# Two column sets of the first mixing stage as seven block products, with their sums on the POOL queue and VectorE

## What is computed

```
h = rmsnorm(x, g_mix[l])
p = h @ w_in[l]                                  # 1024 -> 5632 columns
gates = sigmoid(p[..., OFF_G:]).reshape(b, s, 3, 1024)
y_f = fourier_mix(p[..., OFF_F:OFF_B], w_fourier[l])
y_c = short_conv(p[..., OFF_B:OFF_C], p[..., OFF_C:OFF_V], p[..., OFF_V:OFF_P], w_conv[l], w_conv_out[l])
y_p = pool_mix(p[..., OFF_P:OFF_G], w_pool[l], pool_scale[l])     # (...) * scale
x = x + (gates[:, :, 0] * y_f + gates[:, :, 1] * y_c + gates[:, :, 2] * y_p) @ w_o[l]
```

## Time and profile before

| | us |
|---|---|
| median of 3 runs | 2215.95 (2215.57 to 2216.9) |
| the profiled execution, device time | 2217.72 |
| its span, first to last instruction | 2215.9 |
| first mixing stage, layer 0 and layer 1 | 175.3 and 175.0 |

### The profile page before, as it was taken

One profiled execution on the slowest core, in us unless ns is written; L12 is line 12 of the kernel. 1 busy time (PEld: TensorE's weight loads), 2 busy tenths in 40 slices (PEclk: granted clock), 3 DMA queues, 4 the chain that ended last, 5 costly groups with the idle time before them and its releaser, 6 DMA issues.

```text
span 2215.9 us, 28791 instructions
## 1 busy us (share of the span) xinstructions
PE 2208.1 (100%) x11494; PEld 1886.2 (85%) x11494; DVE 1729.2 (78%) x2163; ACT 1321.5 (60%) x1489; POOL 56.0 (3%) x68
## 2 busy tenths in 40 slices
PE   9999999999999999999999999999999999999999
PEld 8888888888888888888888888888888888788887
DVE  7887566888788566788888799768788887976787
ACT  6566445556556544666656676555565667754555
POOL 0000000000000000000000000000000000000000
PEclk9999999999999999999999999999999999999999
DMA  7977555977879556698597753549778785345876
GB/s 274 327 224 259 166 185 186 310 224 234 287 245 273 187 172 208 215 300 236 193 321 239 236 171 118 204 160 325 231 234 277 239 261 195 105 162 195 287 244 185
DMA packets 170950, 503.86 MB, mean 227 GB/s; under 512 B 18720, under 2 KB 23328, under 8 KB 162624
## 3 DMA queue, kind: packets, MB, share of 16 engines
q1 hardware_dynamic: 161456, 434.90, 55.1%
q0 software_dynamic: 9216, 67.11, 15.4%
q10 hardware_dynamic: 144, 0.00, 0.0%
HBM read 500.91 MB, written 1.05 MB: 227 GB/s over the span
## 4 chain that ended last, share of the span: by engine, by line
PE 90%; DVE 4%; DMA 4%; ACT 1%; issue 1%; SPq 0%; ACTq 0%; DVEq 0%
PE psum L756 24%; PE psum L757 12%; PE psum L692 12%; PE psum L694 12%; PE psum L693 12%; PE psum L888 4%; PE psum L892 4%; PE psum L890 4%; DMA raw<-t_gate_up_1a_dram 2%; DVE split_w L1843 2%; PE psum L724 2%; DMA raw<-t_gate_up_2a_dram 1%; PE psum L1115 1%; DVE gate_up L1983 1%; ACT split_w L1315 0%
## 5 line engine op out<-in xcount | busy, mean ns | idle before, releaser
L1843 DVE TENSOR_TENSOR split_w<-raw,split_w 128x2048 fp32r<-128x2048 f32 (+3 forms) x389 | 842.5, 2177 | 147.4 <-ACT split_w L1315 145.2
L1315 ACT ACTIVATE split_w<-raw 128x2048 fp32r<-128x2048 f32 (+3 forms) x389 | 708.5, 1830 | 291.4 <-PE psum L694 58.4
L756 PE MATMUL psum<-xt,split_w 128*128 128x512 f32 x2464 | 860.1, 393 | 0.5 <-DVE split_w L1843 0.3
L757 PE MATMUL psum<-xt,split_w 128*128 128x256 f32 x2464 | 690.3, 280 | 0.0
L756 PEld LDWEIGHTS psum<-xt,split_w 128*128 128x128 f32 x2464 | 461.2, 187 | 104.0 <-issue 0.6
L757 PEld LDWEIGHTS psum<-xt,split_w 128*128 128x128 f32 x2464 | 465.7, 189 | 0.5
L692 PE MATMUL psum<-split_w,xt 128*128 128x512 f32 (+1 forms) x736 | 289.5, 393 | 0.0
L694 PE MATMUL psum<-split_w,xt 128*128 128x512 f32 (+1 forms) x736 | 283.7, 385 | 0.0
L693 PE MATMUL psum<-split_w,xt 128*128 128x512 f32 (+1 forms) x736 | 283.6, 385 | 0.0
L1983 DVE TENSOR_TENSOR gate_up<-psum,low 128x512 f32<-128x512 f32 x176 | 120.7, 686 | 98.3 <-ACT low L1392 98.1
L692 PEld LDWEIGHTS psum<-split_w,xt 128*128 128x128 f32 x736 | 138.3, 188 | 28.9 <-issue 3.0
(11 more groups left out here) (309 smaller groups left out, 2871.6 us busy)
## 6 DMA issues: line engine op xcount, KB each, us to landing
raw<-w_in_dram SPq DMA_DIRECT2D x180, 512.0 KB, 4.5
raw<-t_gate_up_1b_dram SPq DMA_DIRECT2D x88, 512.0 KB, 6.5
raw<-t_gate_up_2a_dram SPq DMA_DIRECT2D x88, 512.0 KB, 5.9
raw<-t_gate_up_2b_dram SPq DMA_DIRECT2D x88, 512.0 KB, 6.1
raw<-t_gate_up_1a_dram SPq DMA_DIRECT2D x84, 512.0 KB, 6.8
left_sums<-ffn_w_down_quarters_dram POOLq DMA_DIRECT2D x24, 1024.0 KB, 10.0
raw<-ffn_w_down_quarters_dram SPq DMA_DIRECT2D x48, 512.0 KB, 4.4
left_sums<-w_a_quarters_dram POOLq DMA_DIRECT2D x12, 1024.0 KB, 11.0
```

The costliest lines, as they stand in the source:

```text
L756: nc.tensor.matmul(bank, whi[:, slot, w], xt[:, c, :, :], start=c == 0, stop=False)
L757: last = nc.tensor.matmul(bank[:, 0:T], wlo[:, slot, w], xt_hi[:, c, :], start=False, stop=c == DC - 1)
L1315: nc.scalar.activation(whi[:, e.unit(u) % HL, 0:n], raw[:, r, 0:n], ACT.Copy).then_inc(hi_done, 1)
L1843: nc.vector.tensor_tensor(wlo[:, e.unit(u) % HL, 0:n], raw[:, r, 0:n], whi[:, e.unit(u) % HL, 0:n], ALU.subtract).then_inc(w_ready, 1)
```

## The change

Two pairs of 512 columns are each computed as one set of seven block products: set 0 is C with V, set 1 is the second half of the Fourier gate with the second half of the pooling gate. The left blocks are token halves by even or odd chunk of 128 rows; the right blocks are the four quarters "11", "21", "22", "12" of the column pair by odd or even chunks, laid out by the host as `w_in_quarters`. Each product is 12 matmuls into one bank.

- Token sums: DVE forms four sums of the activations (`token_sums`) after the stage's fourth split, ACT takes their high part, DVE the low part.
- Weight sums: POOL loads quarter 11 into `set_left` and adds 12 (U); it loads 12 into `set_right` and adds 22 (T3). DVE forms T2 = U + 22 and T4 = T2 + 21 in `set_left` out of the ring's buffers (`set_sum`), which for 21 must stay until T4 is made: SP's load of the unit after next waits for `set_summed`.
- PSUM snapshots: ACT copies bank 0 after products 11, T2 and T3 (e1, e2, e3) and bank 1 after U (u); DVE combines them (`quarter_added`, `snapshots_apart`, `quarter_apart`).
- The pooling scale is multiplied into the pooling weights before their split (`pool_weights`) in place of the merge.
- The order is new: B before the sets, set 0, pooling and convolution gates, set 1, and the output projection by halves of its rows, both column halves for each. The stage has 38 units per layer in place of 32, of which 30 pass through the ring in place of 32.

The diff, cut to its core:

```diff
+SETS = ({name: 9 + i for i, name in enumerate(("11", "U", "T2", "21", "T3", "22", "T4"))},
+        {"11": 25, "U": 26, "T2": 27, "21": 28, "T3": 29, "22": 30, "T4": 32})
-MIX_UNITS = {1: 32, 2: 36}
+MIX_UNITS = {1: 38, 2: 36}
...
+                wide(w_in, u0, OFF_F)                                  # SP, mix1_loads
+                wide(w_in, u0 + 2, OFF_P)
+                wide(w_in, u0 + 4, OFF_B)
...
+                wide(w_in, u0 + 6, OFF_G)
+                fourier(u0 + 8, 0)
+                for q in ("11", "21", "22"):
+                    set_load(u0 + set_unit(0, q), q, 0)
+                plain(w_in, D, 0, OFF_G + 2 * D, u0 + 16)
+                eng.wait_ge(set_summed, summed(e, 0, "T4"))
+                plain(w_in, D, 4 * P, OFF_G + 2 * D, u0 + 17)
+                pooling(u0 + 18, 0)
+                wide(w_in, u0 + 19, OFF_G + D)
+                convolution(u0 + 21, 0)
+                wide(w_in, u0 + 22, OFF_G + D + 512)
+                convolution(u0 + 24, 1)
+                for q in ("11", "21", "22"):
+                    set_load(u0 + set_unit(1, q), q, 1)
+                pooling(u0 + 31, 1)
+                eng.wait_ge(set_summed, summed(e, 1, "T4"))
+                fourier(u0 + 33, 1)
+                for k in range(2):
+                    for n in range(2):
+                        plain(flat(a["w_o"]), D, 4 * P * k, 512 * n, u0 + 34 + 2 * k + n)
...
+                def product(n, name):                                  # PE
+                    out = psum[:, bank_of(name), :]
...
+                    for i in range(DC // 2):
+                        hi, lo = left(name, i)
...
+                        nc.tensor.matmul(out, hi, whi[:, slot, w], start=start, stop=False, skip_group_check=True)
+                        nc.tensor.matmul(out, hi, wlo[:, slot, w], start=False, stop=False, skip_group_check=True)
+                        last = nc.tensor.matmul(out, lo, whi[:, slot, w], start=False, stop=stop, skip_group_check=True)
...
+                branch_out(u0 + 8, 2, (fq_hi, fq_lo), 0)
+                product(0, "11")
+                eng.wait_ge(done, e.after(done, ("s",)))
+                product(0, "U")
+                eng.wait_ge(acted, e.after(acted, ("e1", 0)))
+                product(0, "T2")
...
+                product(0, "21")
+                eng.wait_ge(acted, e.after(acted, ("e2", 0)))
+                product(0, "T3")
...
+                product(0, "22")
+                eng.wait_ge(acted, e.after(acted, ("e3", 0)))
+                product(0, "T4")
...
+                wide(u0 + 19, 0, XT)
+                eng.wait_ge(done, e.after(done, ("merged", 0, "p")))
+                eng.wait_ge(done, e.after(done, ("bz", 1)))
+                conv_out(u0 + 21)
...
+                out_chunks(u0 + 34, 0, 0)
+                out_chunks(u0 + 34, 0, 1)
+                eng.wait_ge(done, e.after(done, ("merged", 1, "p")))
+                out_chunks(u0 + 35, 1, 0)
+                eng.wait_ge(done, e.after(done, ("merged", 1, "f")))
                 turns("mt1", merged1)
+                out_chunks(u0 + 35, 1, 1)
...
+                split(u0 + 9)                                          # ACT
+                set_sum_split(0, "U")
...
+                nc.scalar.activation(rt[:, :], rt[:, :], ACT.Sigmoid)
+                set_sum_split(0, "T2")
+                gate(0, "f", 1, u0 + 7)
+                split(u0 + 12)
+                snapshot("e1", 0, "11", z[:, 0, :])
+                set_sum_split(0, "T3")
+                snapshot("u", 0, "U", sigs[:, 1, 1, :])
+                split(u0 + 14)
+                snapshot("e2", 0, "T2", sigs[:, 1, 0, :])
+                set_sum_split(0, "T4")
+                split(u0 + 16)
+                snapshot("e3", 0, "T3", sigs[:, 0, 1, :])
+                split(u0 + 17)
+                eng.wait_ge(done, e.after(done, ("wp", 0)))
+                split(u0 + 18)
+                split(u0 + 19)
...
+                for n in range(2):                                     # POOL, set_sums
+                    if n == 0:
+                        eng.wait_ge(done, e.after(done, ("s",)))
+                    else:
+                        eng.wait_ge(w_ready, units(e, u0 + 20, RAW))
+                    load(set_left, "11", n, set_left_in)
+                    add(set_left, "12", n, set_left_added)
+                    if n == 0:
+                        eng.wait_ge(small, e.after(small, ("pl", 1)))
+                    load(set_right, "12", n, set_right_in)
+                    add(set_right, "22", n, set_right_added)
...
+                set_sum_split(0, "U")                                  # DVE
+                set_sum(0, "T2")
...
+                set_sum_split(0, "T2")
+                split(u0 + 12)
+                set_sum_split(0, "T3")
+                set_sum(0, "T4")
+                split(u0 + 14)
+                set_sum_split(0, "T4")
+                quarter_added(0, z[:, 0, :])
+                split(u0 + 16)
+                snapshots_apart(0)
+                quarter_apart(0)
...
+                split(u0 + 17)
+                pool_weights(0)
...
+                merge(0, "f", True, 4, sig1)
+                split(u0 + 18)
+                split(u0 + 19)
...
+                split(u0 + 20)
...
+                merge(0, "p", False, 4, sig1)
+                split(u0 + 21)
```

More of the change, by code:

```diff
@@ L562, in mix1_loads @@
[L562 to L571, removed]
@@ L1030, in mix1_tensor @@
[L1030 to L1038, removed]
-                eng.wait_ge(done, e.after(done, ("merged", 1, "c")))
+                product(1, "11")
@@ new lines, in mix1_scalar @@
+                split(u0 + 23)
+                eng.wait_ge(done, e.after(done, ("merged", 0, "p")))
+                gate(0, "c", 0, u0 + 20)
+                split(u0 + 24)
+                split(u0 + 25)
+                set_sum_split(1, "U")
+                eng.wait_ge(done, e.after(done, ("merged", 0, "c")))
+                gate(1, "c", 1, u0 + 23)
+                set_sum_split(1, "T2")
+                split(u0 + 28)
+                snapshot("e1", 1, "11", sigs[:, 0, 0, :])
+                set_sum_split(1, "T3")
@@ new lines, in mix1_scalar @@
+                eng.wait_ge(done, e.after(done, ("x11", 1)))
+                sigmoid(sigs[:, 1, 1, :], sigs[:, 1, 1, :], 1)
+                split(u0 + 34)
+                eng.wait_ge(done, e.after(done, ("x01", 1)))
+                sigmoid(sigs[:, 1, 0, :], sigs[:, 1, 0, :], 0).then_inc(acted, e.mark(acted, ("sig", 1, "p")))
+                for j in range(2):
+                    turned_hi(mt1_hi, ("mt0", j), 6 + j, 2 * j)
+                split(u0 + 35)
+                multiplied(u0 + set_unit(1, "T4"))
@@ L1571, in mix1_scalar @@
[L1571 removed]
+                split(u0 + 40)
             def mix2_scalar(u0):
@@ new lines, in mix1_vector, with merge @@
+                set_sum(0, "T2")
+                def merge(n, branch, first, y, sig):
+                    merged = (ptok, merged1)[n]
+                    for m in range(MT):
+                        if first:
+                            ins = nc.vector.tensor_tensor(merged[:, m, :], psum[:, y + m, :], sig[:, m, :], ALU.mult)
+                        else:
+                            e.link(nc.vector.tensor_tensor(part1[:, :], psum[:, y + m, :], sig[:, m, :], ALU.mult))
+                            ins = nc.vector.tensor_tensor(merged[:, m, :], merged[:, m, :], part1[:, :], ALU.add)
+                        if m == 0:
+                            e.link(ins)
+                    ins.then_inc(done, e.mark(done, ("merged", n, branch)))
+                    eng.wait_ge(done, e.after(done, ("merged", n, branch)))
```

401 lines of the change are left out of this document (265 added, 136 removed).

## The result

The changed kernel takes 2221.43 us (median of 6 runs, 2220.1 to 2226.73) against 2215.76 us (2213.71 to 2216.9): ratio 1.0027, 95% interval 1.0017 to 1.0037. It is slower by some 5.7 us. The forecast was 2207.0, with a range of 2204.5 to 2213.0; the time lies outside it, and on the other side of the kernel before. The profiled execution took 2224.71 us, with a span of 2222.8.

The account below looks back on a forecast made before the run. PE was taken to bound the stage, other engines having slack. 48 matmuls fewer save 10.9 us, less 2 x 1.0 of stalls gives 8.9: 2208.8 us profiled, 2207.0 as a median, range 2204.5 to 2213.0.

Parts of the forecast that it names:

- has more room: Second set: T2 ready at 309 where PE wants it at 314.3, T4 at 326.1 for 327.6.
- 4.5 us: Second set: time the load of quarter 22 takes, its start possible once unit 24 is split at 297.7.
- wants it at 331.8. I count 0.3 us: Output projection: first half ready at 331.3 where PE wants it at 331.8, with a stall of 0.3 us.
- 48 matmuls less: Products of both column sets in two layers: seven instead of eight, at 0.2267 us per matmul, saving 10.9 us.
- VectorE's 32 us more per layer: Added subtractions, sums and small operations take VectorE to about 140 of 170 us, on average hidden by PE.
- ScalarE's 17: Seven conversions and eight bank copies, less one copy: 17 us more per layer, on average hidden by PE.
- The first set: Walked in layer 0: U's slot free at 236.0, 0.4 us of stall counted, POOL sums ready at 231 and 244.
- no margin: Convolution: VectorE ends at 287.1 where PE reaches the convolution's output at 287.0; 0.3 us of stall counted.
- Rivals 2 and 3: Left sums moderately late, 2212.7 us, chance 0.08; both transfers near the worst rows, 2224 us, chance 0.06.
- Rival 1: VectorE decides from T3 to the convolution, 2 us more per layer: 2211 us, chance 0.22.
- signs I gave for "wrong": U's conversion waiting for a DMA, several us of wait at convolution or output projection, or wider spacing in the product.
- sign I gave for "right": Both POOL adds landed before the conversions of U and T3 ask, listed among other signs.

Follow-up runs that it names:

- no_pool1: Changed kernel without the second set's four POOL transfers in both layers: 2209.13 us, ratio 0.9966 to the kernel before.
- spread: Changed kernel with three second-set POOL transfers, each where the ring has room, and VectorE adding quarter 11 to the left: 2209.64 us, 0.9972 of the kernel before.
- no_pool0: Changed kernel without the first set's four POOL transfers in both layers: 2221.91 us, ratio 1.0024 to the kernel before.
- early: Changed kernel with the second set's four POOL transfers started at the split of the first set's T4, five ring units earlier: 2223.9 us.
- right_first: Changed kernel with the second set's right POOL pair started at the split of the first set's T3, left pair at T4's: 2218.43 us.
- spread_wo: Changed kernel with the edits of spread and late_wo together: 2207.09 us, ratio 0.9957 to the kernel before.
- sp_free: Changed kernel with second-set T4 summed from T2 and T3, and SP no longer waiting for that sum: 2222.48 us, 1.0026 of the kernel before.
- u_on_dve: Like right_first, but POOL loads only quarter 12 for the second set's U and VectorE adds the ring's quarter 11: 2223.8 us.
- late_wo: Changed kernel with first merged half taken before unit 34's split and T4's sigmoid before unit 35's: 2217.21 us, 1.0006 of the kernel before.

## Why the prediction was wrong

**The step that failed** is that the second set "has more room", with quarter 22's load at "4.5 us". The 4.5 us is a median of ring loads, which in this stage had no transfer of POOL beside them (DMA 0.56). I walked POOL's transfers of set 1 nowhere: I asked of the first set's whether they land in time, and of the second's not even that, and of neither what they do to the ring. They start at the split of unit 20, run beside the quarters, and these take 11.6 us. T2's sum ended at 311.6 for a PE that wanted T2 at 314.3, with ScalarE and VectorE still to go: 1.7 us of stall there, 1.6 at the next products, then the fourth sum done at 324.0 for my 318.6 and the output projection's wait of 2.9. I had 0.3 us for all of this. The engine time of an adding transfer, twice that of a plain one (below), was missing too; the page of the kernel before would have given it.

**A second, smaller step**: "wants it at 331.8. I count 0.3 us" at the output projection. With the quarters on time (no_pool1, spread) it still waited 1.0 to 1.6 us per layer, since ScalarE converted unit 35 ahead of the sigmoid that the first half needs, and idled 2.0 us for unit 34's load before that. I had counted the load and the splits, not the order of ScalarE's queue.

**What held.** 48 matmuls less (11494 to 11446), at the same spacing in the new product line (12 of them in 2.72 us from 308.75). VectorE's 32 us more per layer: 62.4 us over two layers. ScalarE's 17: 31.1 over two. The first set went as walked: U's conversion was released by PE at 235.75 (236.0), one stall of 0.2 us at quarter 22 (0.4), both POOL sums hidden, which no_pool0 confirms. They landed at 232.8 and 247.0 for my 231 and 244, and the second only 0.7 us ahead of its conversion, so that was close. The convolution was on time with "no margin", and early and right_first show that there was none. What the 48 matmuls are worth stands: spread_wo is 10.2 us below the kernel before on its chip, where I had 8.9 with 2 us of stalls left.

**The rivals.** None was this one. Rivals 2 and 3 had POOL's sums late in the first set; what came was the ring late in the second, through the same engines. Rival 1, VectorE, was full only because it had started late. Of the signs I gave for "wrong", the wait at the output projection came (2.9 and 1.8 us). The one of ScalarE waiting for a DMA came at another place than I named: U's conversion waited for PE, that of quarter 11 in the second set 9.08 us for its load. The sign I gave for "right", both POOL adds landed in time, came as well: it says nothing of what they delay.

**The account**, in the profiled executions: 10.9 us saved, 11.6 waited in the two second sets, about 1.7 lost to the clock (below): 2.4 slower, of 6.9. By the turns of x in PE's timeline the two stages grew by 4.0 us (182.1 to 186.1) and 1.3 us (182.2 to 183.5). Most of the difference lies in the stalls themselves, which the view of waits gives too short. The stall before T2 in PE's timeline:

```profile
313.97 0.39 PE L1071 MATMUL psum<-split_w,mt_lo 128*128 128x512 f32 x1
316.06 0.47 PE L1069 MATMUL psum<-split_w,mt_hi 128*128 128x512 f32 x1 [1.71 <-DVE split_w L2043]
```

The two starts are 2.09 us apart in place of 0.23, so 1.86 are lost where the view says 1.71, and the next start follows after 0.31. Summed by starts, the stalls of both stages cost some 14 us, 2 more than by the view, which makes 4.8 of the 5.3. A further 1.9 us passed in the first feed-forward part of the second block (181.1 us before, 183.0 after), and 0.3 were gained ahead of the first stage. That feed-forward part took 180.7 us in spread_wo, 181.7 in sp_free and 183.8 in no_pool0, so it doesn't go with late quarters alone; no run here was made for it, and its cause stays open.

## What to carry to other kernels

Before a transfer is counted as hidden, look at whom it delays: list the loads with a deadline that are in flight beside it, and give them the duration of a full DMA, not the median of a quiet one. A late transfer is then moved to where the ring is idle (here 302 to 317 us), not simply started earlier. Whether it also pays to cut one (a plain load and 2.2 us of VectorE for an adding transfer) depends on where the rest stand: with the same cut u_on_dve lost and spread won. Before a stage's critical operands are walked, write down the queue order of each engine, since a conversion that waits for a load holds up whatever stands behind it.

## What the runs showed of the hardware

**An adding transfer costs the DMA engines about twice a plain one.** In spread, the right load alone on POOL's queue (250 to 258 us) moved 1.05 MB in 37.4% of the engines, 8 us x 0.374 = 3.0 us of all 16; the add of the same size (285 to 312) took 27 x 0.207 = 5.6 us. The ring's loads there cost 27 x 0.474 / 4.44 = 2.9 us per MB. So set 1's four transfers, two of each kind, are more than the 12 us of four plain ones: in the changed kernel they took 35.5 x 0.428 = 15.2 us (the first line below, 279 to 314.5 us). The other two lines are the DMA view of 250 to 258 us in spread:

```profile
q0 software_dynamic: 576, 4.19, 42.8%
```
```profile
q0 software_dynamic: 144, 1.05, 37.4%
set_right<-w_in_quarters_dram POOLq DMA_DIRECT2D x1, 1024.0 KB, 5.1
```

The page of the kernel before already had this price. All that POOL's queue (q0) carried there were the 64 adding transfers of 1.05 MB: 2215.9 x 0.154 / 67.1 = 5.1 us of all engines per MB, against 2215.9 x 0.551 / 434.9 = 2.8 on SP's queue (q1):

```profile
q1 hardware_dynamic: 161456, 434.90, 55.1%
q0 software_dynamic: 9216, 67.11, 15.4%
```

The plain load of spread, for which the trace of before had no row, took 5.1 us from issue to landing where I had put 7. The Trainium skill's fit (DMA: Bandwidth & Descriptors, Anatomy of one DMA), an estimate of 4.4 us, was nearer. In the changed kernel the four plain loads of layer 0 took 5.2, 8.6, 6.8 and 14.4 us, the longest beside an adding transfer and six ring loads, so neither figure could stand for all of them.

**A stall can cost more than its length.** After PE had stood idle in layer 0 (335.5 to 338.7 us), the granted clock went from its full 2.4 GHz to the lower level of 1.2 GHz for most of the next 4 us, worth 2 x 0.48 + 2 x 0.37 = 1.7 us. Stretches of the changed kernel, columns as above:

```profile
336.00:338.00 2.00, 0.00 (x0) 0.00 (x0) 2.00 (x4) 2.00 (x3) 0.00 (x0) 1.00 0.47 106
338.00:340.00 2.00, 1.32 (x6) 1.13 (x7) 1.93 (x3) 2.00 (x2) 0.00 (x0) 1.00 0.79 268
340.00:342.00 2.00, 2.00 (x7) 1.52 (x6) 1.93 (x3) 0.23 (x1) 0.00 (x0) 0.52 0.65 247
342.00:344.00 2.00, 2.00 (x7) 1.60 (x6) 1.97 (x3) 0.00 (x0) 0.00 (x0) 0.63 0.00 0
```

In early, PE idle for most of 290 to 294 us is followed by 0.50, 0.50 and 0.53 from 294 to 300. Layer 1 of the changed kernel, with a longest stall of 2.0 us, kept 1.00. But layer 0 of late_wo, behind a stall of 1.9 us, did not:

```profile
314.00:316.00 2.00, 0.91 (x3) 0.81 (x4) 1.97 (x3) 2.00 (x3) 0.00 (x0) 0.86 0.00 0
316.00:318.00 2.00, 2.00 (x6) 1.54 (x6) 1.97 (x2) 2.00 (x3) 0.00 (x0) 0.50 0.00 0
```

So the length of a stall alone does not tell here whether the clock falls behind it. My prediction priced every stall at its length.
